# Two engines take a copy out of PSUM at another place of their queues in the fused attention stage

## The reference, cut to what matters

```
z = q @ k.T / sqrt(d) + bias                     # causal: only keys before the query
log_1mb = where(causal, log_sigmoid(-z), 0)
later = reverse cumsum(log_1mb) - log_1mb        # over the keys behind this one
w = where(causal, exp(log_sigmoid(z) + later), 0)
out = w @ v
```

## Time and profile before

| what | value |
|---|---|
| median of 3 runs | 3705.56 us (3702.88 to 3705.97) |
| profiled execution | 3709.2 us |
| its span | 3707.4 us |
| PE busy | 3474.8 us, 94% |
| DVE busy | 1908.7 us, 51% |
| ACT busy | 1189.1 us, 32% |
| issues of page loads (two groups) | 256 each, 512.0 KB each, 5.7 and 5.8 us to landing |
| key copies on ACT, line 818 | 256 of 645 ns |
| key copies on DVE, line 659 | 256 of 683 ns |

### The profile page before, as it was taken

How to read it: one execution, slowest core, us unless ns; L and a number is a source line. 1 busy time by engine, 2 the same in 40 slices (tenths; PEclk the granted TensorE clock), 3 DMA queues, 4 the chain that set the end, 5 groups by cost and what they waited for, 6 DMA issues and landing times. The chain is left out here.

```text
span 3707.4 us, 66686 instructions
## 1 busy us (share of the span) xinstructions
PE 3474.8 (94%) x25746; PEld 2929.0 (79%) x25746; DVE 1908.7 (51%) x2982; ACT 1189.1 (32%) x2509; POOL 606.6 (16%) x678
## 2 busy tenths in 40 slices
PE   8988999999789999999998999889978999999998
PEld 8976777776667988889996778456767888888897
DVE  3147866665676444444445457446157744444445
ACT  2136666665321211111125344331233211111112
POOL 0001111110102111111112111018221311111113
PEclk9999999999889999999999999999988999999999
DMA  4169999999030111111113100139523111111111
GB/s 142 51 224 373 385 391 392 391 391 372 9 130 12 46 46 36 43 45 44 35 57 108 46 22 25 30 124 343 185 87 103 35 46 45 45 42 37 45 45 71
DMA packets 188714, 472.87 MB, mean 128 GB/s; under 512 B 31561, under 2 KB 129734, under 8 KB 152599
## 3 DMA queue, kind: packets, MB, share of 16 engines
q1 hardware_dynamic: 168646, 449.65, 33.3%
q10 hardware_dynamic: 19824, 19.92, 1.7%
HBM read 449.61 MB, written 19.91 MB: 127 GB/s over the span
## 5 line engine op out<-in xcount | busy, mean ns | idle before, releaser
L2005 DVE TENSOR_TENSOR x<-x,f_d 128x512 f32<-128x512 f32 x540 | 368.4, 687 | 304.6 <-PE f_d L1819 249.5
L1980 POOL TENSOR_TENSOR f_hl<-f_h,f_hh 128x364 fp32r<-128x364 f32 (+1 forms) x192 | 178.7, 932 | 1251.9 <-ACT f_hh L1938 1251.8
L2025 DVE TENSOR_TENSOR f_h<-f_h 128x364 f32<-128x364 f32 (+1 forms) x192 | 105.6, 552 | 512.9 <-ACT f_h L1932 512.9
L1819 PE MATMUL f_d<-f_w2l,f_hh 128*128 128x512 f32 x896 | 354.4, 396 | 0.0
L1819 PE MATMUL f_d<-f_w2h,f_hl 128*128 128x512 f32 x896 | 354.4, 395 | 0.0
L1819 PE MATMUL f_d<-f_w2h,f_hh 128*128 128x512 f32 x896 | 354.3, 395 | 0.0
L1932 ACT ACTIVATE f_h<-up 128x364 f32<-128x364 f32 (+1 forms) x192 | 90.6, 473 | 537.7 <-PE up L1698 536.3
L1698 PE MATMUL up<-xH,w1h 128*128 128x364 f32 (+1 forms) x768 | 254.1, 331 | 5.4 <-ACT f_h L1932 5.4
L1698 PE MATMUL up<-xL,w1h 128*128 128x364 f32 (+1 forms) x768 | 253.3, 330 | 0.0
L1698 PE MATMUL up<-xH,w1l 128*128 128x364 f32 (+1 forms) x768 | 253.2, 330 | 0.0
L1698 PE MATMUL up<-xH,f_w1l 128*128 128x364 f32 (+1 forms) x768 | 252.2, 328 | 0.0
(11 more groups left out here) (603 smaller groups left out, 7829.8 us busy)
## 6 DMA issues: line engine op xcount, KB each, us to landing
x<-in_cache_sb_kv SPq DMA_DIRECT2D x256, 512.0 KB, 5.7
ss_kv<-in_cache_sb_kv SPq DMA_DIRECT2D x256, 512.0 KB, 5.8
w<-in_ffn_w SPq DMA_DIRECT2D x64, 1024.0 KB, 5.2
mp_qb<-mp_q SPq DMA_DIRECT2D x24, 1024.0 KB, 8.3
mp_vc<-in_cache_dil_kv ACTq DMA_DIRECT2D x9, 1024.0 KB, 5.7
pe_raw<-in_w_in_even SPq DMA_DIRECT2D x8, 1024.0 KB, 7.9
mp_kc<-in_cache_dil_kv SPq DMA_DIRECT2D x8, 1024.0 KB, 11.0
group_w<-in_w_in_odd SPq DMA_DIRECT2D x3, 2048.0 KB, 8.6
```

The costliest lines, as they stand in the source:

```text
L1819: mm = pe.matmul(out, a, b, start=(n == 0), stop=(n == len(parts) - 1))
L1980: low = lambda dst, n0, n1, at: g.tensor_tensor(dst, h[:, u % HSLOTS, n0 - at:n1 - at], hh[:, c % 2, f, n0:n1].bitcast(F32), ALU.subtract)
L2005: v.tensor_tensor(K.x[0:r, t, cs], K.x[0:r, t, cs], dn_b[(c * DOWN + u) % 4][0:r, :], ALU.add).then_inc(added, 1)
L2025: v.tensor_tensor(x, x, x, ALU.mult).then_inc(squared, 1)
```

## The change

In odd steps, where PE does prompt values, both engines take their copy of the turned prompt weights earlier. ACT does it between its key copies 0 and 2 and no longer behind the copy of the sample weights. DVE does it ahead of its key copy 1 and no longer between key copies 1 and 3. Even steps keep their order, and what is copied, by whom and with which waits stays as it is.

```diff
# DVE's loop
+                    due = t - 2 < NU and copier(t - 2) == 1
+                    if due and t % 2 == 1:
+                        prompt_copy(t - 2)
                     if g < NSTEP:
                         copy_keys(g, 1)
-                    if t - 2 < NU and copier(t - 2) == 1:
+                    if due and t % 2 == 0:
                         prompt_copy(t - 2)
                     if g < NSTEP:
                         copy_keys(g, 3)
# ACT's loop
+                    due = t - 2 < NU and copier(t - 2) == 0
                     if g < NSTEP:
                         copy_keys(g, 0)
+                    if due and t % 2 == 1:
+                        prompt_copy(t - 2)
+                    if g < NSTEP:
                         copy_keys(g, 2)
                     if g >= 1:
                         copy_weights(g - 1)
-                    if t - 2 < NU and copier(t - 2) == 0:
+                    if due and t % 2 == 0:
                         prompt_copy(t - 2)
```

## The result

The changed kernel takes 3674.07 us (median of 4, 3672.88 to 3676.87) against 3705.76 us before (4 runs): the ratio is 0.9918, with a 95% interval from 0.9903 to 0.9933. Run once more beside three of the experiments it was 3676.09 against 3711.36 us, ratio 0.9899 (0.9884 to 0.9915). By the medians the change is 31.7 and 35.3 us faster. The forecast was 39 us and 3666.5 us, with a range from 3661 to 3680.

A forecast was written before the change was run, and what follows sets the result against it. The prediction took PE's queue, with its gap ahead of the prompt values, as the bound. 41.5 - 0.6 - 1.5 = 39.4, rounded 39 us, takes the median from 3705.56 to 3666.5 us; range of eight in ten 3661 to 3680.

The forecast's parts named there:

- The bound before: Steps 1 to 120: PE's queue sets the step's length, its one regular gap being ahead of the prompt values; 43.3 us.
- ACT's half at no cost: ACT's moved copy fits into 0.28 us of idle time ahead of key copy 2; otherwise 8 us at most.
- DVE's half: Odd steps with DVE units: copy moved ahead of key copy 1 ends the "issue" waits, 17.4 us, leaving 0.07 in three-tile steps.
- the one-tile case: Odd steps with a one-tile prompt block: sample values come no earlier than 0.86 behind line 528; four steps lose 0.7 us.
- What step 31 gains is lost at step 32: DVE's scan in step 32 has no idle time before it, so 0.6 us is given back; bounds 0 to 5.
- The sum of PE's order: PE's gaps of 43.3 us less 0.7 and 1.1 leave 41.5 us, less 0.6 given back at step 32.
- The pages' pace: SP's four loads need 4.95 us against a mean step of 5.08; short steps lose 1.5 us, bounds 0 and 10.
- A: Rival: the page loads become the bound, step 5.16 us, gain 31 us, 3674 us; chance 0.10.
- Its stronger form: Page loads give no more than 388 GB/s, nothing gained, 3703 to 3706 us; chance 0.05 together with D.
- B: Rival: line 588's "issue" waits are not DVE's copy, so only ACT's half goes: 22 us, 3683 us; chance 0.06.
- C: Rival: moved copies wait at the head of ACT's and DVE's queues, 16 us slower, 3721 us; chance 0.02.
- D: Rival: no change, PE's gap merely moves to the sample values; chance 0.05 together with the hard limit of A.

The follow-up runs named there:

- e2: Changed kernel with DVE's order put back to that of before, so only ACT's half stays: 3688.07 us, ratio 0.9936, 128 steps of 664.3 us.
- e10: Changed kernel, but ACT takes its copy in odd steps behind key copy 2, still ahead of the sample weights: 3682.98 us, ratio 0.9931.
- e9: Kernel before the change, with page numbers written in and half the rows loaded from step 4 on: 3706.48 us, ratio 0.9990, 128 steps of 686.6 us.
- e7: Changed kernel with page numbers written in and half the rows of each page loaded from step 4 on: 3671.62 us, ratio 0.9899.
- e1: Changed kernel with ACT's order put back to that of before, so only DVE's half stays: 3693.94 us, ratio 0.9955, 128 steps of 670.7 us.
- e3: Changed kernel with page numbers written into the program instead of read from the table: 3673.89 us, ratio 0.9902.
- e4: Changed kernel loading only the key half of each page from step 4 on: 3695.99 us, ratio 0.9965.
- e8: Changed kernel with page numbers read as before, but half the rows of each page loaded from step 4 on: 3669.38 us, ratio 0.9888.
- e6: Changed kernel with a step's page numbers read ahead of the slot wait and without their bounds check: 3677.20 us, ratio 0.9909.
- e5: Changed kernel where SP reads a step's four page numbers ahead of its wait for the slot: 3677.86 us, ratio 0.9910.

## Why the prediction was right, and where it was off

*The bound before.* Right. Without any limit from the loads the kernel before was 0.6 us faster in its 128 steps, and 3706.48 against 3710.04 us in time.

*ACT's half at no cost.* Right: key copies 0 and 2 keep their distance, line 837 follows 0.42 behind line 528 as before, and e2 gives 22.9 us where the sum had 23.8 less losses. e10 shows that the place counts.

*DVE's half.* Right. In step 23 after the change the moved copy and the values stand so:

```profile
355.40 0.56 DVE L703 TENSOR_TENSOR ss_pwT<-ss_to,ss_seen 128x384 f32<-128x384 f32 x1
...
355.69 0.38 PE L528 MATMUL ss_zw<-ident,ss_w 128*128 128x128 f32 x2
...
356.06 0.88 PE L588 MATMUL ss_to<-ss_pwT,v_sb 128*64 128x128 f32 x12
```

The values start 0.37 behind line 528; the sum had 0.38 (0.31 at best and 0.07 left over). In step 69, the one-tile case, the sample values start 0.86 behind line 528 (592.89 to 593.75), as reckoned. DVE's half alone brought 16.4 us, where I had expected 17.

*What step 31 gains is lost at step 32.* Right, and to the size, by a neighbour of the instruction that was named. PE waits in step 32 not for the scan of the earlier trace rows but for DVE's addition of prompt outputs just ahead of it (line 713), which stands behind the factor work in DVE's full queue: 0.25 before the change (the first fence) and 0.84 after it (the second), 0.59 more.

```profile
411.68 0.52 PE L576 MATMUL ss_to<-ident,ss_pz 128*128 128x128 f32 x3 [0.25 <-DVE xT L713]
```

```profile
400.87 0.52 PE L576 MATMUL ss_to<-ident,ss_pz 128*128 128x128 f32 x3 [0.84 <-DVE xT L713]
```

*The sum of PE's order.* 41.5 less 0.6 was forecast. Measured without the loads' limit it is 40.6 (e9 to e7), 0.3 from the forecast and within the noise. Of all comparisons this one bears out the mechanism most directly.

*The pages' pace.* This term was mis-sized, and it is all of the error that the 128 steps show. I took 1.5 us within bounds of 0 and 10. The loads cost 7 to 9 us after the change and 0.6 before, so 6 to 8. Two things were wrong in that step. I took SP's issues (4.95 us for four) as the limit and reckoned with PE's mean step of 5.08 above it. Where the loads are really pressed, what binds is their own rate: at the end of the stage with fixed pages, where SP has time to spare, it is 422 GB/s, so 4.97 us for a step's 2.1 MB. The two limits lie so near each other that this mistake alone costs little. In the whole stage after the change the loads already run at 399 to 415 GB/s, most of the way to that rate, although most steps are PE's own. The slices of the changed kernel (GB/s, 40 for the span; the stage fills the fourth to the ninth):

```profile
GB/s 143 51 228 399 403 415 412 415 412 272 14 120 12 46 46 46 46 46 46 44 37 109 47 27 24 27 162 365 131 94 98 35 46 46 46 46 38 42 46 72
```

The second mistake is the one that cost: a mean above the limit does not protect single steps. Those of 4.8 to 4.9 us in a row use up the lead. After the change the trace names six waits for pages between 240 and 830 us, and eight between 850 and 890, these three among them:

```profile
851.40 1.06 PE L508 MATMUL ss_tk<-ident,x 128*128 128x128 f32 x8 [0.26 <-DMA x<-in_cache_sb_kv]
...
857.16 1.06 PE L508 MATMUL ss_tk<-ident,x 128*128 128x128 f32 x8 [1.03 <-DMA x<-in_cache_sb_kv]
...
882.80 1.06 PE L508 MATMUL ss_tk<-ident,ss_kv 128*128 128x128 f32 x8 [1.00 <-DMA ss_kv<-in_cache_sb_kv]
```

The last seven steps take 36.4 us in the changed kernel, 34.2 before, and 33.5 with half the bytes. So the end of the stage lost about 2 us where 1 was reckoned, and the steps ahead of it some 5 where I had put half a microsecond. The named waits for pages behind the first steps add up to 5.3 us, 4.4 more than before, where the prediction had less than 3. For the remaining 2 to 3 us the trace names no wait, but they lie near the others: of the steps 2 to 127, laid beside those of e7, the changed kernel is longer by more than 0.04 us in 34 (8.6 us in all), gathered around steps 45 to 48, 57 to 65, 87 to 95 and 115 to 127.

*The rivals.* A, that the loads become the bound, came about in part, at a fifth of the gain. In its numbers it came closer than the forecast: it had 31 us, 3674 us, about 408 GB/s and a step of 5.16, and measured were 31.7 us and 3674.07 us by the medians, 410, and 654.0 / 127 = 5.15 (the second measurement's 35.3 us lies halfway between A and the forecast). The forecast's own range from 3662 to 3672 was missed; the time lies in the wider one that includes A. What speaks against A as the mechanism is that it wanted the loads to bind through the whole stage, while 92 of 126 steps agree within 0.04 us with those without the loads' limit. Its stronger form, that loads cannot go faster than the 388 GB/s of before, is refuted by 410. The Trainium skill, "DMA: Bandwidth & Descriptors", section "Where 436 GB/s comes from", has 435 GB/s for the fabric and says that for loads from HBM the figure of about 358 for each core binds. The traces agree with the first as a ceiling not quite reached (422 over a step at most) and not with the second on this lone core. B fell with e1. C did not occur: neither moved copy has a wait on line 576. D did not occur either: the sample values' waits on line 837 stayed at 4.7 us in 10 steps. I had expected four more of these; the one-tile steps are not among the ten, although in step 69 the start comes at the reckoned 0.86.

## What to carry to other kernels

When one engine waits for a copy, look in the copying engine's own queue for idle time ahead of something that is not ready yet: the copy costs nothing there, while one place further on it cost 11 of ACT's 23 us in PE's order, and 4 to 6 us of the time, since the loads hid the rest. Before adding up gaps, ask what is the next bound in every step, not on the mean, and take the rate of the transfers from a stretch where they are really pressed (here the last steps of the kernel before already showed it: they wait for pages at 4.96 to 4.98 us a step). And when two edits each gain alone but less together, take the suspected common resource away from both kernels: that separates what the edit is worth from what the resource takes back.

## What the runs showed of the hardware

The loads of one core (512 KB each, in four slots) rose with the change from 388 to 410 GB/s between 240 and 880 us, and the landing from a median of 5.7 to 6.3 us; asked for as early as slots allow, they landed after 7.8 us and moved 411 GB/s (e3). Four issues on SP with a page number read into a register take 4.95 us, so 1.24 each, of which the transfer instruction itself is 0.475; for half a page in twice as many pieces it is 0.543 (e4), and in as many pieces still 0.475 (e8). Leaving out the bounds check (e6 against e5) raised SP's waits for slots from 6.6 to 138.9 us, and the steps came only to the changed kernel's length.
